# Two hybrid mixers: the second half's choice of keys cut in two round a recurrence step, later steps and splits in another order

## The chip, the cores and the metric

The kernel runs on one core of a Trainium2 chip. The core has five engines that run their own instruction streams and meet at semaphores: TensorE (PE, matmuls and transposes), VectorE (DVE), ScalarE (ACT), GpSimd (POOL) and SyncE (SP, which here only starts DMAs). The metric is the time of one execution in microseconds, lower is better; the figure compared is the median over runs.

## The reference

Two layers over 256 tokens of width 1024. Each layer has a mixer and a feed-forward part (dense SwiGLU in layer 0, top 2 of 8 experts in layer 1). The mixer projects the normed input, and feeds three branches whose outputs are gated and added:

```
proj = h @ w_in[layer]
a_u, a_b, a_c, s_u, q, k, v, qi, ki, wi, gates = split_columns(proj)
y_a = short_conv_mixer(a_u, a_b, a_c, conv_w[layer]) @ w_out_a[layer]
y_b = s5_mixer(s_u, ...) @ w_out_b[layer]              # diagonal complex recurrence, GELU, GLU
y_c = dsa_mixer(q, k, v, qi, ki, wi, ...) @ w_out_c[layer]
g = jax.nn.sigmoid(gates.reshape(Bsz, L, N_BRANCH, D_MODEL))
x = x + (g[:, :, 0] * y_a + g[:, :, 1] * y_b + g[:, :, 2] * y_c) @ w_o[layer]
```

In `dsa_mixer` a light indexer scores all keys for each query, the 64 best of the causal ones are chosen (`lax.top_k`), and attention with 8 heads runs over the chosen keys only. The kernel does this with a bias of -1e30 on keys that are not chosen.

## The kernel before

**Weights.** All weights pass as float32 chunks of 1 MB through three steps: SyncE loads a chunk into `raw` (6 buffers), ScalarE copies it to `w_hi` in TensorE's fp32r format (line 259, 3 buffers), and VectorE subtracts to get the rest `w_lo` (line 264). TensorE multiplies each chunk three times (hi by hi, lo by hi, hi by lo; lines 619 to 621, or 643 to 645 where channels stand on the partitions). A mixer has 35 chunks, numbered 0 to 34. Chunk n's matmuls wait for `lo_done` of n, ScalarE's copy waits for `used` of n - 3. "The split of chunk n" below is VectorE's instruction of line 264.

**Recurrence.** The S5 branch runs in 8 steps, q = 0 to 7. In each, TensorE makes the inputs (`bu`, lines 742 and 744; waits for `scanned` of step q - 1), VectorE rotates and scans them (`rotate_in`, called `turn_q`, lines 1634 to 1642; waits for the inputs, the step's table and the output of step q - 2), GpSimd rotates back (`rotate_out`, lines 2214 to 2217) and in mixer 0 then makes the table of step q + 2 (lines 2184 to 2190; in mixer 1 it loads it), and TensorE makes the outputs (`y_of`, lines 760 to 769; waits for `rotated`). `BU_AT` and `Y_AT` say behind which chunk TensorE places inputs and outputs of each step; at one chunk the output comes first. The last index in a list is step 7.

**Attention.** For each of two blocks of 128 queries VectorE searches the 64th best score in 8 rounds (`best`, lines 1707 and 1709), then marks the chosen keys and turns the marks into a bias in `keybias` (`choose`, lines 1717 to 1726, nine instructions). Four groups i = 0 to 3 (block i // 2, four heads each) go through `logits` (TensorE, line 810), `shift` (VectorE, lines 1740 to 1744; adds the bias), `softmax_exp` and `normalise` (ScalarE, lines 1248 and 1257, with VectorE's `invert_sums` between, line 1749), `turn_probs` (TensorE's transposes, line 822), `copy_pT` (ScalarE, line 1263), `values` (TensorE, line 833) and `copy_o` (ScalarE, line 1270).

**Gates.** `sigmoid_gate` (ScalarE, line 1241) puts a gate's half into `gate`, `merge_gate` (VectorE, line 1760) multiplies it with a branch's output. The tile `h_tok` holds the normed input, then the heads of q and k until they are turned (line 779), and from `merge_gate(layer, 0, ...)` on the merged output. For block 1, `best` and `choose` work in three rows of 256 columns: before, in the second half of `gate`.

**What sets the order.** Nothing but the code: each engine runs its instructions in the order in which the function of its block issues them. The functions `mixer` of TensorE, ScalarE and VectorE interleave chunk work with the steps above.

## Time and profile before

| | us |
|---|---|
| runs shown, median of 3 | 1796.02 (1794.18 to 1797.77) |
| profiled execution | 1792.95 |
| its span, first to last instruction | 1791.2 |
| TensorE busy | 1709.4 (95%) |
| VectorE busy | 1387.1 (77%) |
| ScalarE busy | 1069.8 (60%) |
| GpSimd busy | 394.3 (22%) |
| mean granted clock of TensorE | 0.979 of full speed |

Mixer 0 lies at about 0 to 287 us of the span, the dense part behind it, mixer 1 from about 490 to 740 us, and the experts from there to the end. Their second halves, from chunk 14 on, start at 129 and 617 us. The chain of work that ended last is 82% TensorE and 13% VectorE.

In a timeline row the columns are the start in us, the duration in us, engine, line, operation, tiles out and in, shapes and count; in brackets the engine's idle time before it and who ended it. VectorE's and TensorE's instructions overlap a little with the next, so the cost of a piece is taken from start to start.

### The profile page before, as it was taken

The numbers are of one execution on the slowest core, as the hardware profiler recorded it, in microseconds if no ns is written. First come the engines' busy times: TensorE is split into PE (matmuls) and PEld (weight loads), VectorE is DVE, ScalarE is ACT, GpSimd is POOL, SyncE is SP. The second block draws the span as 40 slices with busy tenths as digits, with TensorE's granted clock in tenths as the row PEclk, the third lists the DMA queues.
The fourth block names the chain that finished last, engine by engine and source line by source line (L and its number), as shares of the span: only waits on it lengthen the run. The fifth ranks groups of instructions, "written<-read, shape, count | busy, mean of one in ns | idle before, by whom it ended". The sixth has DMA issues, their size and how long they took to land.

```text
span 1791.2 us, 24481 instructions
## 1 busy us (share of the span) xinstructions
PE 1709.4 (95%) x9030; PEld 1446.3 (81%) x9030; DVE 1387.1 (77%) x1172; ACT 1069.8 (60%) x878; POOL 394.3 (22%) x492
## 2 busy tenths in 40 slices
PE   7898998999979989979999999999999999999998
PEld 5886887999868878767888888888888888888886
DVE  6987565455459875657888898898898988989987
ACT  5343454544343444446777777777777777777775
POOL 8978300899024332000000000000000000000000
PEclk9998999999989989979999999999999999999999
DMA  8432365556543434647999999999999999999995
GB/s 313 146 100 94 124 202 165 187 171 216 158 153 119 124 106 135 204 140 259 380 376 348 385 343 369 382 339 385 369 350 381 363 350 380 355 376 366 349 376 188
DMA packets 210840, 475.76 MB, mean 266 GB/s; under 512 B 7728, under 2 KB 32432, under 8 KB 210528
## 3 DMA queue, kind: packets, MB, share of 16 engines
q1 hardware_dynamic: 207456, 463.34, 73.1%
q0 software_dynamic: 2896, 11.01, 1.7%
q8 instruction: 36, 0.59, 0.1%
q10 hardware_dynamic: 432, 0.65, 0.1%
q14 instruction: 20, 0.16, 0.0%
HBM read 471.30 MB, written 3.67 MB: 265 GB/s over the span
## 4 chain that ended last, share of the span: by engine, by line
PE 82%; DVE 13%; issue 2%; ACT 2%; POOL 1%; DMA 0%; DVEq 0%; ACTq 0%; POOLq 0%
PE ps L619 24%; PE ps L621 23%; PE ps L620 23%; DVE w_lo L264 4%; PE ps L643 1%; PE ps L1073 1%; PE ps L644 1%; PE ps L645 1%; DVE x_tok L2077 1%; PE ps L742 1%; PE ps L744 1%; PE ps L767 1%; PE ps L685 1%; ACT w_hi L259 1%; PE ps L769 1%
## 5 line engine op out<-in xcount | busy, mean ns | idle before, releaser
L264 DVE TENSOR_TENSOR w_lo<-raw,w_hi 128x2048 fp32r<-128x2048 f32 (+1 forms) x439 | 1009.9, 2309 | 266.2 <-ACT w_hi L259 264.7
L259 ACT ACTIVATE w_hi<-raw 128x2048 fp32r<-128x2048 f32 (+1 forms) x439 | 839.5, 1915 | 377.6 <-PE ps L621 358.4
L619 PE MATMUL ps<-w_hi,xg_hi 128*128 128x512 f32 x896 | 358.2, 400 | 3.3 <-issue 1.4
L621 PE MATMUL ps<-w_hi,xg_lo 128*128 128x512 f32 x896 | 350.6, 391 | 0.0
L620 PE MATMUL ps<-w_lo,xg_hi 128*128 128x512 f32 x896 | 350.1, 391 | 0.0
L619 PE MATMUL ps<-w_hi,hT_hi 128*128 128x256 f32 (+2 forms) x672 | 228.1, 339 | 2.3 <-DVE hT_lo L1604 2.3
L620 PE MATMUL ps<-w_lo,hT_hi 128*128 128x256 f32 (+2 forms) x672 | 224.2, 334 | 0.0
L621 PE MATMUL ps<-w_hi,hT_lo 128*128 128x256 f32 (+2 forms) x672 | 224.1, 333 | 0.0
L619 PE MATMUL ps<-w_hi,hidT_hi 128*128 128x512 f32 x536 | 209.7, 391 | 2.8 <-DVE hidT_lo L1918 2.8
L621 PE MATMUL ps<-w_hi,hidT_lo 128*128 128x512 f32 x536 | 208.8, 390 | 0.0
L620 PE MATMUL ps<-w_lo,hidT_hi 128*128 128x512 f32 x536 | 208.7, 389 | 0.0
L619 PEld LDWEIGHTS ps<-w_hi,xg_hi 128*128 128x128 f32 x896 | 169.0, 189 | 43.4 <-DVE w_lo L264 8.6
L621 PEld LDWEIGHTS ps<-w_hi,xg_lo 128*128 128x128 f32 x896 | 168.7, 188 | 36.7
L620 PEld LDWEIGHTS ps<-w_lo,xg_hi 128*128 128x128 f32 x896 | 169.2, 189 | 32.9
L2316 POOL DMA_INDIRECT xg_tok<-table_store,token_of x7 | 18.8, 2679 | 783.2 <-DVE token_of L2041 783.2
L619 PEld LDWEIGHTS ps<-w_hi,hT_hi 128*128 128x128 f32 x672 | 128.1, 191 | 17.8 <-DVE hT_lo L1604 3.2
L621 PEld LDWEIGHTS ps<-w_hi,hT_lo 128*128 128x128 f32 x672 | 128.0, 191 | 12.3
L620 PEld LDWEIGHTS ps<-w_lo,hT_hi 128*128 128x128 f32 x672 | 128.3, 191 | 11.0
L619 PEld LDWEIGHTS ps<-w_hi,hidT_hi 128*128 128x128 f32 x536 | 100.7, 188 | 23.7 <-DVE hidT_lo L1918 3.3
L621 PEld LDWEIGHTS ps<-w_hi,hidT_lo 128*128 128x128 f32 x536 | 100.6, 188 | 21.1
L620 PEld LDWEIGHTS ps<-w_lo,hidT_hi 128*128 128x128 f32 x536 | 100.7, 188 | 20.3
L643 PE MATMUL ps<-hT_hi,w_hi 128*128 128x256 f32 x256 | 75.3, 294 | 6.3 <-DVE w_lo L264 6.3
(331 smaller groups left out, 2022.1 us busy)
## 6 DMA issues: line engine op xcount, KB each, us to landing
raw<-moe_w SPq DMA_DIRECT2D x336, 1024.0 KB, 7.2
raw<-w_in SPq DMA_DIRECT2D x44, 1024.0 KB, 5.4
raw<-ffn_w SPq DMA_DIRECT2D x33, 1024.0 KB, 5.3
raw<-w_o SPq DMA_DIRECT2D x8, 1024.0 KB, 5.0
raw<-w_out_a SPq DMA_DIRECT2D x4, 1024.0 KB, 5.0
raw<-w_out_c SPq DMA_DIRECT2D x4, 1024.0 KB, 5.0
raw<-w_out_b SPq DMA_DIRECT2D x4, 1024.0 KB, 5.0
raw<-w_in SPq DMA_DIRECT2D x4, 904.0 KB, 7.1
```

What stands on the lines that cost most here:

```text
L259: act.activation(w_hi[:, n % SPLIT, 0:width], raw[:, n % RAW, 0:width], ACT.Copy).then_inc(hi_done, 1)
L264: dve.tensor_tensor(w_lo[:, n % SPLIT, 0:width], raw[:, n % RAW, 0:width], w_hi[:, n % SPLIT, 0:width].bitcast(F32), ALU.subtract).then_in ...
L619: pe.matmul(dst, x_hi, hi, start=first, stop=False, skip_group_check=True)
L620: pe.matmul(dst, x_hi, lo, start=False, stop=False, skip_group_check=True)
L621: return pe.matmul(dst, x_lo, hi, start=False, stop=last, skip_group_check=True)
L643: pe.matmul(dst, wh, x_hi[:, k0 + k, :], start=start, stop=False, skip_group_check=True)
L644: pe.matmul(dst, wl, x_hi[:, k0 + k, :], start=False, stop=False, skip_group_check=True)
L645: mm = pe.matmul(dst, wh, x_lo[:, k0 + k, :], start=False, stop=last and k == 3, skip_group_check=True)
L685: tr = pe.transpose(ps[:, bank + k // 2, at:at + P], src[:, b, k * P:k * P + P], ident[:, :])
L742: pe.matmul(dst, ba[r:r + 32, c, part, :], u2[:, 0, :], start=part == 0 and jj == 0, stop=False, skip_group_check=True, tile_position=(r, 0))
L744: mm = pe.matmul(dst, b_rows[r:r + 32, c, part, :], u2[:, 1, :], start=False, stop=True, skip_group_check=True, tile_position=(r, 0))
L2316: pool.indirect_dma_start(xg_tok[:, :], None, h_rows, bass.IndirectOffsetOnAxis(token_of[:, 0:1], 0))\
```

## The change

The choice of block 1 is cut in two: `choose` keeps its first six instructions, and the last three move to a new function, `bias_of_choice`. Step 3 of the recurrence and the split of chunk 16 stand between them. Inputs and outputs of later steps go one or two chunks back on TensorE (tables `BU_AT`, `Y_AT`); the turned probabilities of groups 2 and 3 go behind another chunk or another step; ScalarE does two more splits and a gate ahead of softmax 2; the three choice rows of block 1 move from `gate` to `h_tok`, and with them the first search waits for `qkT_ps` (all heads turned) where it waited for `rope_done`. Both mixers run the same code.

```diff
-BU_AT = (10, 12, 13, 14, 15, 16, 17, 18)
-Y_AT = (13, 14, 15, 16, 17, 18, 19, 20)
+BU_AT = (10, 12, 13, 14, 16, 17, 19, 20)
+Y_AT = (13, 14, 15, 17, 19, 20, 21, 22)
...
 (TensorE, mixer)
                 rows(c0 + C_OA, 0, yac_hi, yac_lo, True, False, gates_read=6 * layer + 2)
-                turn_probs(layer, 2)
                 s5(C_OA)
                 rows(c0 + C_OA + 1, 2, yac_hi, yac_lo, False, True, block0=S["branch_block0"])
+                turn_probs(layer, 2)
+                s5(C_OA + 1)
                 values(layer, 2)
                 logits(layer, 3)
-                s5(C_OA + 1)
...
                 stripe(C_GC, 0, 1)
+                s5(C_GC + 1)
                 turn_probs(layer, 3)
-                s5(C_GC + 1)
...
 (ScalarE, mixer)
                 sp(16)
-                softmax_exp(layer, 2)
-                normalise(layer, 2)
                 sp(17)
                 sigmoid_gate(layer, C_GA + 2, 1, 1)
                 sp(18)
+                softmax_exp(layer, 2)
+                normalise(layer, 2)
+                sp(19)
                 copy_pT(layer, 2)
-                sp(19)
+                sp(20)
                 copy_o(layer, 2)
+                sp(21)
                 softmax_exp(layer, 3)
-                sp(20)
                 normalise(layer, 3)
-                sp(21)
+                sp(22)
                 copy_pT(layer, 3)
                 sigmoid_gate(layer, C_GC, 2, 0)
-                sp(22)
                 copy_o(layer, 3)
...
 (VectorE)
-                return (gate[:, r // 2, HALF + SEQ * (r % 2):HALF + SEQ * (r % 2 + 1)] for r in range(1, 4))
+                return (h_tok[:, 0, SEQ * r:SEQ * (r + 1)] for r in range(1, 4))
...
-                    dve.wait_ge(S["rope_done"], BLOCKS * (layer + 1))
+                    dve.wait_ge(S["qkT_ps"], 2 * (layer + 1))
...
                 own.then(dve.scalar_tensor_tensor(work, work, smalls[:, 1:2], eq, ALU.is_le, ALU.mult))
+
+            def bias_of_choice(b):
+
+                keys = (b + 1) * P
+                sc = keybias[:, b, 0:keys]
+                work, gt, _ = choice_rows(b)
                 own.then(dve.tensor_tensor(work, work, gt, ALU.add))
                 own.then(dve.tensor_scalar(sc, work, -NEG, NEG, ALU.mult, ALU.add))
...
                 choose(0)
+                bias_of_choice(0)
...
                 chunk(15)
-                choose(1)
-                chunk(16)
-                shift(layer, 2)
                 dve.wait_ge(S["ya_hi_done"], layer + 1)
                 sub_hi(flat(yac_lo[:, :, :]), flat(u_t[:, :, :]), flat(yac_hi[:, :, :]), S["ya_lo_done"])
+                choose(1)
+                turn_q(3)
+                chunk(16)
+                bias_of_choice(1)
+                shift(layer, 2)
+                chunk(17)
                 invert_sums(layer, 2)
-                turn_q(3)
-                chunk(17)
                 turn_q(4)
                 chunk(18)
                 add_skip(layer, 0)
                 add_skip(layer, 1)
+                merge_gate(layer, 0, C_OA)
                 turn_q(5)
-                merge_gate(layer, 0, C_OA)
+                chunk(19)
                 shift(layer, 3)
-                chunk(19)
+                chunk(20)
                 invert_sums(layer, 3)
+                chunk(21)
                 turn_q(6)
-                chunk(20)
+                chunk(22)
                 turn_q(7)
-                chunk(21)
-                chunk(22)
```

TensorE in mixer 0 behind the matmuls of chunk 15, before: the last output matmuls of step 2, then step 4's input matmuls (L742, L744), then chunk 16 (L619 on).

```order
L767 MATMUL ps<-state,ca 32x128
L769 MATMUL ps<-state,par_sb 32x128
L742 MATMUL ps<-su,ba 128x128 [waits scanned]
L744 MATMUL ps<-su,par_sb 128x128
L742 MATMUL ps<-su,ba 128x128
L744 MATMUL ps<-su,par_sb 128x128
L742 MATMUL ps<-su,ba 128x128
L744 MATMUL ps<-su,par_sb 128x128
L742 MATMUL ps<-su,ba 128x128
L744 MATMUL ps<-su,par_sb 128x128
L619 MATMUL ps<-w_hi,yac_hi 128x512 [waits lo_done,ya_lo_done,gate_done]
```

The same place of the changed kernel.

```order
L767 MATMUL ps<-state,ca 32x128
L769 MATMUL ps<-state,par_sb 32x128
L619 MATMUL ps<-w_hi,yac_hi 128x512 [waits lo_done,ya_lo_done,gate_done]
L620 MATMUL ps<-w_lo,yac_hi 128x512
L621 MATMUL ps<-w_hi,yac_lo 128x512
```

Step 4's input matmuls, which wait for step 3's scans, now stand behind the 24 matmuls of chunk 16.

VectorE in mixer 0 behind the split of chunk 15, before: the nine choice instructions, the split of chunk 16, then shift 2 (L1740 on).

```order
L264 TENSOR_TENSOR w_lo<-raw,w_hi 128x2048 [waits hi_done]
L1717 TENSOR_SCALAR gate<-keybias,top 128x256
L1718 TENSOR_SCALAR gate<-keybias,top 128x256
L1719 TENSOR_REDUCE row_sb<-gate 128x1 [waits dve_step]
L1720 SCALAR_TENSOR_TENSOR gate<-ones,gate 128x256
L1721 TENSOR_SCALAR row_sb<-row_sb 128x1 [waits dve_step]
L1722 SCALAR_TENSOR_TENSOR gate<-gate,row_sb 128x256 [waits dve_step]
L1723 TENSOR_TENSOR gate<-gate 128x256 [waits dve_step]
L1724 TENSOR_SCALAR keybias<-gate 128x256 [waits dve_step]
L1726 TENSOR_TENSOR keybias<-keybias,causal 128x128 [waits dve_step]
L264 TENSOR_TENSOR w_lo<-raw,w_hi 128x2048 [waits hi_done,dve_step]
L1740 SCALAR_TENSOR_TENSOR probs<-ps,keybias 128x512 [waits logit_ps]
```

VectorE in the changed kernel, from the sixth choice instruction on (L1722): step 3 (L1634 to L1642), the split of chunk 16, then the last three choice instructions (now L1729 to L1732).

```order
L1722 SCALAR_TENSOR_TENSOR h_tok<-h_tok,row_sb 128x256 [waits dve_step]
L1634 TENSOR_TENSOR qkT<-ps,table 128x4x128 [waits y_ps,bu_ps,table_done,dve_step]
L1635 TENSOR_TENSOR ps<-ps,table 128x512 [waits dve_step]
L1636 TENSOR_TENSOR ps<-qkT,ps 128x256 [waits dve_step]
L1637 TENSOR_TENSOR ps<-qkT,ps 128x256
L1642 SCALAR_TENSOR_TENSOR qkT<-trig,ps 128x128 [waits dve_step]
L1642 SCALAR_TENSOR_TENSOR qkT<-trig,ps 128x128 x3
L264 TENSOR_TENSOR w_lo<-raw,w_hi 128x2048 [waits hi_done]
L1729 TENSOR_TENSOR h_tok<-h_tok 128x256
L1730 TENSOR_SCALAR keybias<-h_tok 128x256 [waits dve_step]
L1732 TENSOR_TENSOR keybias<-keybias,causal 128x128 [waits dve_step]
```

Step 3 stood behind the choice, the split, shift 2, the split of y_a (`sub_hi`) and `invert_sums`; now only the split of y_a and six choice instructions stand between chunk 15's split and it.

ScalarE in mixer 0 behind the copy of chunk 16, before and then in the changed kernel.

```order
L259 ACTIVATE w_hi<-raw 128x2048 [waits used,raw_full4]
L1248 ACT_TABLE_LOAD
L1248 ACTIVATE probs,row_sb<-probs,row_sb 128x256 [waits shifted]
L1248 ACTIVATE probs,row_sb<-probs,row_sb 128x256 x3
L1257 ACTIVATE probs<-probs,row_sb 128x256 [waits row_inv_done]
L1257 ACTIVATE probs<-probs,row_sb 128x256 x3
L259 ACTIVATE w_hi<-raw 128x2048 [waits used,raw_full5]
```

```order
L259 ACTIVATE w_hi<-raw 128x2048 [waits used,raw_full4]
L259 ACTIVATE w_hi<-raw 128x2048 [waits used,raw_full5]
L1241 ACTIVATE gate<-ps 128x2x512 [waits used]
L259 ACTIVATE w_hi<-raw 128x2048 [waits used,raw_full0]
L1248 ACT_TABLE_LOAD
L1248 ACTIVATE probs,row_sb<-probs,row_sb 128x256 [waits shifted]
```

The copies of chunks 17 and 18 no longer stand behind softmax 2.

## Rows read from the trace of the kernel before

**Rows 1.** Timeline of TensorE, mixer 0, chunks 15 and 16.

```profile
136.65 0.49 PE L742 MATMUL ps<-su,ba 32*128 32x128 f32 x2
...
138.66 0.50 PE L619 MATMUL ps<-w_hi,hT_hi 128*128 128x512 f32 x1
...
144.34 0.41 PE L767 MATMUL ps<-state,ca 128*32 128x128 f32 x2
...
153.74 0.79 PE L742 MATMUL ps<-su,ba 32*128 32x128 f32 x2 [7.47 <-DVE qkT L1642]
...
165.30 1.03 PE L822 MATMUL ps<-ident,probs 128*128 128x128 f32 x8
```

**Rows 2.** Timeline of TensorE, mixer 1, chunk 16 and behind chunk 17.

```profile
639.34 0.79 PE L742 MATMUL ps<-su,ba 32*128 32x128 f32 x2 [5.19 <-DVE qkT L1642]
...
650.47 1.04 PE L822 MATMUL ps<-ident,probs 128*128 128x128 f32 x8
...
661.00 1.58 PE L833 MATMUL ps<-probs,v_sb 128*64 128x128 f32 x16
...
664.12 0.72 PE L760 MATMUL ps<-su,k 128*128 128x128 f32 x4
```

**Rows 3.** Stretches: length, busy us by engine, granted clock, DMA share, GB/s.

```profile
153.70:162.30 8.60, 8.56 (x27) 7.28 (x28) 6.84 (x10) 4.11 (x3) 8.16 (x7) 0.50 0.36 122
...
74.00:81.00 7.00, 4.99 (x25) 5.02 (x26) 6.76 (x14) 2.04 (x2) 6.84 (x9) 0.54 0.56 180
123.50:130.00 6.50, 6.50 (x48) 5.52 (x49) 4.93 (x8) 5.34 (x4) 4.18 (x2) 1.00 0.17 27
```

**Rows 4.** Timeline of VectorE, mixer 0, behind chunk 15, and the two skips.

```profile
135.16 0.81 DVE L1717 TENSOR_SCALAR gate<-keybias,top 128x256 f32<-128x256 f32 x1
...
138.83 1.29 DVE L1723 TENSOR_TENSOR gate<-gate 128x256 f32<-128x256 f32 x1
...
142.13 2.66 DVE L264 TENSOR_TENSOR w_lo<-raw,w_hi 128x2048 fp32r<-128x2048 f32 x1
144.72 1.27 DVE L1740 SCALAR_TENSOR_TENSOR probs<-ps,keybias 128x512 f32<-128x512 f32 x2
...
147.74 1.21 DVE L1782 TENSOR_TENSOR yac_lo<-u_t,yac_hi 128x1024 fp32r<-128x1024 f32 x1
...
150.08 0.69 DVE L1634 TENSOR_TENSOR qkT<-ps,table 128x512 f32<-128x512 f32 x1
...
153.72 2.29 DVE L264 TENSOR_TENSOR w_lo<-raw,w_hi 128x2048 fp32r<-128x2048 f32 x1
...
168.24 0.87 DVE L1649 SCALAR_TENSOR_TENSOR su<-su,par_sb,ps 128x256 f32<-128x256 f32 x2 [4.80 <-PE ps L769]
```

**Rows 5.** Timeline of VectorE, mixer 1, the choice of keys.

```profile
622.87 1.27 DVE L1717 TENSOR_SCALAR gate<-keybias,top 128x256 f32<-128x256 f32 x1
...
627.36 0.42 DVE L1723 TENSOR_TENSOR gate<-gate 128x256 f32<-128x256 f32 x1
...
628.47 2.29 DVE L264 TENSOR_TENSOR w_lo<-raw,w_hi 128x2048 fp32r<-128x2048 f32 x1
```

**Rows 6.** Timeline of TensorE, mixer 0, three earlier short waits.

```profile
72.11 1.06 PE L779 MATMUL ps<-ident,h_tok 128*128 128x128 f32 x8 [2.48 <-POOL h_tok L2234]
...
76.01 0.55 PE L643 MATMUL ps<-hT_hi,w_hi 128*128 128x256 f32 x1 [2.84 <-DVE w_lo L264]
...
123.49 1.14 PE L810 MATMUL ps<-qkT 64*128 64x256 f32 x8 [1.61 <-ACT qkT L1270]
```

**Rows 7.** Timeline of GpSimd, mixer 0, end of the table of step 3.

```profile
137.52 0.99 POOL L2190 TENSOR_TENSOR table<-pool_t 128x256 f32<-128x256 f32 x1
```

**Rows 8.** Timeline of ScalarE, mixer 0, the probabilities of group 2.

```profile
150.18 1.70 ACT L1257 ACTIVATE probs<-probs,row_sb 128x256 f32<-128x256 f32 x4 [0.24 <-DVE row_sb L1749]
```

**Rows 9.** Timelines of ScalarE and VectorE, mixer 0, the search of block 1.

```profile
84.19 0.38 ACT L1355 ACTIVATE qkT<-ps 128x256 f32<-128x256 f32 x1 [8.15 <-PE ps L779]
...
85.62 0.42 DVE L1707 MAX8 top<-keybias 128x8 f32<-128x256 f32 x1
```

## The prediction

> **What bounds the kernel now.** I read the list of who waited for whom first, then TensorE's own order of time in the second half of both mixers, then the stretches by clock, and last VectorE's order of time behind the two waits found. In the first view the one large wait of TensorE inside the mixers' second half is that of the input matmuls of a recurrence step (line 742) for VectorE's scans (line 1642). It comes once in each mixer, at the same place, before step 4's input matmuls: 7.47 us in mixer 0 [rows 1] and 5.19 us in mixer 1 [rows 2]. Elsewhere there TensorE goes from one piece to the next, so in this half each us of its idle time is a us of the span, and VectorE's load counts only where TensorE asks for something that isn't there.
>
> Each wait has a tail. In mixer 0 the matmuls from 153.7 to 162.3 run at a granted clock of 0.50, the lower of the two levels, 1.2 GHz; mixer 1 has the same tail, seen by its durations. The price by starts: step 4's input matmuls and chunk 16's 24 matmuls take 165.30 - 153.74 = 11.56 us. Step 3's input matmuls and chunk 15, the same work at 2.4 GHz, take 144.34 - 136.65 = 7.69 us [rows 1]. So the tail costs 3.87 us in mixer 0, and in mixer 1 (650.47 - 639.34) - 7.69 = 3.44 us [rows 2].
>
> **Why TensorE waits there.** It stands before step 4's input matmuls at 153.74 - 7.47 = 146.27, and in mixer 1 at 639.34 - 5.19 = 634.15. VectorE has much before step 3's scans are done. From the end of chunk 15's split at 135.16 it does the choice of keys (to 142.13: 3.67 us for the first six instructions, 3.30 for the last three), chunk 16's split (2.59), shift 2 (144.72 to 147.74: 3.02), the split of y_a (1.21), a wait for ScalarE's exponentials, and step 3 (150.08 to 153.72: 3.64) [rows 4].
>
> **The change part by part.** Times are those of the profiled execution.
>
> Step 4's input matmuls go behind chunk 16, and step 3 on VectorE comes right behind the first six choice instructions. Both old waits go: 7.47 + 5.19 = 12.66 us, and with them both tails, 3.87 + 3.44 = 7.31 us. Together 19.97 us. What is late next?
>
> Mixer 0, chunk 16. TensorE asks for its split at 146.27. VectorE: 135.16, + 1.21 for y_a, + 3.67 for six choice instructions = 140.04, + 3.64 for step 3 = 143.68, + 2.2 to 2.6 for the split = 145.9 to 146.3. The table that step 3 multiplies by ends at 137.52 + 0.99 = 138.51 [rows 7], 1.5 us before it is asked for. So chunk 16 waits 0 to 0.1 us, or 0.8 if the six choice instructions take the 4.49 us of mixer 1 [rows 5]; I take 0.2.
>
> Mixer 0, chunk 17. TensorE asks at 146.4 + 5.68 (24 matmuls, 138.66 to 144.34) + 2.01 (step 4's input matmuls) = 154.1. VectorE goes on from 146.1 with the last three choice instructions (3.30), shift 2 (3.02) and a split (2.2): 154.6. These three took 3.30 us in mixer 0 and 628.47 - 627.36 = 1.11 in mixer 1 [rows 4, 5]; with 1.11 the wait is gone. The most is 3.30 + 3.02 + 2.6 - 7.69 = 1.2, however late chunk 16 was, since TensorE starts it when VectorE has it. I take 0.7.
>
> Mixer 1. VectorE leaves chunk 15's split at 622.87 and needs 1.2 + 4.49 (622.87 to 627.36) + 3.64 + 2.2: 634.4, against 634.15. Wait 0.25. Chunk 17: TensorE asks at 634.4 + 7.69 = 642.1; VectorE has 634.4 + 1.11 + 3.02 + 2.2 = 640.7, or 643.3 with 3.30 for the three and 2.6 for the split. Wait 0 to 1.2; I take 0.15.
>
> New waits in all: 0.2 + 0.7 + 0.25 + 0.15 = 1.3 us, between 0 and 0.8 + 1.2 + 0.65 + 1.2 = 3.9 (the 0.65 is the 0.25 with a split of 2.6). None is near the waits after which the clock fell. Behind a wait of 1.61 us, at 123.49, the clock stays at 1.00, while from 74 to 81, round the second of two waits of 2.48 and 2.84 us, it is 0.54 [rows 3, 6]. So no tail is charged.
>
> Turned probabilities behind chunk 17, and ScalarE's softmax behind chunk 18's split. Before, group 2's probabilities are ready at 150.18 + 1.70 = 151.88 [rows 8] and turned at 165.30: 13.4 us of cover. Shift 2 ends about 4.7 us later than before (152.4 for 147.7), and TensorE comes to the turning about 5 us earlier (154.8 + 5.6 = 160.4). Cover left: 3.7 us, so no cost. ScalarE's two table loads fewer in each mixer lie in its idle time: nothing.
>
> Outputs of steps 3 to 7 and inputs of 5 to 7 move one or two chunks back. They are as many as before and at full clock cost the same. Values of one group and logits of the next, with the small wait between them, are 664.12 - 661.00 = 3.12 us [rows 2], and the wait in it stays. The gate merge ahead of step 5: after chunk 17 TensorE does the turning (0.9), output 3 (1.9), input 5 (2.0) and the 3.12 us, and asks for the merge at about 168.3. VectorE has output 3 at 163.2, two skips in 0.87 and half of the merge, as wide as the split of y_a, in 1.2 [rows 4]: 165.3, cover 3.0. Then merge, step 5 and chunk 19's split end by 172.5 to 172.9; TensorE, past chunk 18, asks at 174.0: cover 1.1 to 1.5. It is the thinnest one left. Later steps have more.
>
> Choice rows in h_tok: the search for the second block's keys now waits for all heads to be turned. ScalarE's copy behind the last turning starts at 84.19, and VectorE gets to the search at 85.62 [rows 9]: 1.4 us of cover, cost nothing. Queued behind that wait are shift 0, the convolution's input and chunk 11's split.
>
> **Sum.** -19.97 + 1.3 = -18.7 us. The profiled execution of 1792.95 us (span 1791.2) becomes 1774.3. Everything behind mixer 1 is moved as a block: TensorE's largest other waits are in the norms and come along. The median of the runs shown lies 3.07 us above the profiled execution, so I forecast 1796.0 - 18.7 = 1777.3 us.
>
> **A rule beside the rows.** The same three choice instructions cost 3.30 us beside GpSimd's table work and 1.11 without it [rows 4, 5], and GpSimd is busy in mixer 0 all through the stretch. The Trainium skill (SBUF — State Buffer, Who interferes with whom) says that a VectorE instruction with two SBUF inputs and a GpSimd instruction that reads SBUF hold one pair of ports in turn, the later one blocked till the first ends. By that rule mixer 1's three instructions, which now follow a split during which GpSimd's rotation stands ready, would be held too: with the 3.30 there the sum would be -18.7 + 1.05 = -17.6 us, 1778.4. No row of before has these instructions at that place, so the trace can't say whether they meet.
>
> **Rivals.**
>
> A. The slowing beside GpSimd comes at each new place, and the waits before chunks 16 and 17 reach their bounds. In mixer 0 that is 0.8 + 1.2 = 2.0 us in two waits one after the other, and such a pair may bring a tail of 3.9 back, as the clock fell behind the pair of 2.48 and 2.84 us. For it: the 1.11 against 3.30. Against it: every instruction would have to meet its worst case. Price in mixer 0: 2.0 - 0.9 + 3.9 = 5.0 us, 1782.3. In both mixers: 1.85 - 0.4 + 3.4 = 4.9 more, 1787.2.
>
> B. The wait only changes its place: step 3 is held by its table or by step 1's output, and TensorE stops as long before chunk 16 as it did before step 4. Then nothing is gained: about 1796. Against it is the table's end at 138.51.
>
> C. Slower: VectorE becomes the bound from chunk 16 to chunk 19. TensorE then meets a wait over 2 us at chunks 16 and 17 of both mixers, and each brings its own tail where before there was one in each mixer. Four times (2.5 + 3.9) = 25.6 us against 19.97 saved: 1801.7. It decides at 20 / 4 - 3.9 = 1.1 us a wait if each had a tail; but at 1.61 us none came, so it needs waits beyond that at all four places, while their bounds are 0.65 to 1.2.
>
> D. No new wait at all and a run at the lower edge of the spread: 1796.0 - 20 - 2 = 1774.
>
> **How the numbers follow.** Forecast, 1774 to 1781: 0.77. A: 0.17. B: 0.03. C: 0.03. D is the forecast's lower edge. The range is 1773 to 1786: it takes in the bounds of the new waits, the runs' spread of 1.8 us to either side, and A in one mixer. What a measurement can tell from no change is 0.2%, 3.6 us. Faster: 0.77 + 0.17 = 0.94; same: 0.03; slower: 0.03.
>
> **What would show it.** In the changed profile no wait before step 4's input matmuls in either mixer; clock 1.00 from chunk 15 to chunk 19; short waits, under 1 us, for VectorE's split of chunk 17 in mixer 0. The stretch from chunk 14 to chunk 23 is shorter by 10.4 us in mixer 0 and 8.2 in mixer 1. The forecast is wrong if a wait over 2 us with a clock of 0.5 stands before chunk 16 or 17, if the wait for the scans reappears at step 5 or 6, or if the dense or expert stage takes another time than before.

## The result and the profile after

| | before | after |
|---|---|---|
| median, us | 1796.25 (1794.18 to 1797.77) | 1777.36 (1776.43 to 1778.07) |
| profiled execution, us | 1792.95 | 1776.91 |
| its span, us | 1791.2 | 1775.2 |
| mean granted clock of TensorE | 0.979 | 0.983 |

The ratio is 0.9894, with a 95% interval of 0.9882 to 0.9905. The median before is here taken over four runs; the forecast started from the 1796.02 of the three shown. The medians differ by 18.9 us; the forecast was 18.7, a median of 1777.3.

The list of who waited for whom, TensorE in the changed kernel. Columns: us in total, times, longest.

```profile
PE ps L685 <- DVE h_tok L1591: 27.3, 4, 10.0
PE ps L643 <- DVE w_lo L264: 6.2, 3, 2.8
...
PE ps L619 <- DVE w_lo L264: 2.6, 5, 1.0
```

The two waits of the input matmuls for the scans (7.47 and 5.19 us, [rows 1, 2]) are gone from it. The last line was 0.5 us in 3 waits before: these are the new waits for VectorE's splits. The first line (the norms) is in both kernels.

TensorE's timeline in the changed kernel, chunk 16 to the turning of group 2's probabilities: mixer 0, then mixer 1.

```profile
147.16 0.47 PE L619 MATMUL ps<-w_hi,yac_hi 128*128 128x512 f32 x1 [1.03 <-DVE w_lo L264]
...
152.78 0.49 PE L742 MATMUL ps<-su,ba 32*128 32x128 f32 x2
...
154.95 0.50 PE L619 MATMUL ps<-w_hi,yac_hi 128*128 128x512 f32 x1
...
160.57 1.04 PE L822 MATMUL ps<-ident,probs 128*128 128x128 f32 x8
...
626.26 0.47 PE L619 MATMUL ps<-w_hi,yac_hi 128*128 128x512 f32 x1 [0.67 <-DVE w_lo L264]
...
631.89 0.49 PE L742 MATMUL ps<-su,ba 32*128 32x128 f32 x2
...
634.43 0.50 PE L619 MATMUL ps<-w_hi,yac_hi 128*128 128x512 f32 x1 [0.47 <-DVE w_lo L264]
```

Step 4's input matmuls (152.78, 631.89) start with no wait, where [rows 1, 2] have 7.47 and 5.19 us. Chunk 16 waits 1.03 and 0.67 us, chunk 17 0.47 us in mixer 1. In mixer 0 it waits about 0.15: from input matmuls to chunk it is 154.95 - 152.78 = 2.17, where 138.66 - 136.65 = 2.01 is the plain length [rows 1]. The new waits add up to 2.3 us.

TensorE's clock in the same stretch of mixer 0 (PEclk, the third number from the end), behind the turnings of the merged output in mixer 0's last part, and in the same stretch of mixer 1.

```profile
147.00:155.00 8.00, 7.75 (x41) 6.36 (x41) 7.83 (x10) 3.48 (x10) 7.61 (x7) 1.00 0.37 131
155.00:163.00 8.00, 8.00 (x46) 6.77 (x47) 5.69 (x10) 4.88 (x7) 7.65 (x8) 1.00 0.50 155
257.00:261.00 4.00, 3.12 (x14) 2.32 (x12) 3.81 (x7) 2.11 (x5) 1.02 (x2) 0.63 0.42 146
626.00:644.00 18.00, 17.28 (x98) 14.47 (x99) 14.99 (x22) 10.29 (x17) 10.01 (x9) 1.00 0.54 173
```

Where [rows 3] have 0.50, there is 1.00. The clock stays at 1.00 from chunk 14 to the GLU in both mixers: both tails are gone with the waits.

**Where the time went.** Starts of the same piece in the two timelines, us:

| piece on TensorE | before | after | earlier by |
|---|---|---|---|
| chunk 14, mixer 0 | 129.08 | 128.94 | 0.14 |
| GLU (first L643 with yb_hi), mixer 0 | 237.84 | 227.38 | 10.46 |
| first chunk of the dense part | 301.27 | 291.58 | 9.69 |
| first chunk of mixer 1 | 511.08 | 501.06 | 10.02 |
| chunk 14, mixer 1 | 616.96 | 608.40 | 8.56 |
| GLU, mixer 1 | 723.02 | 706.84 | 16.18 |
| turning in the last norm | 782.06 | 767.41 | 14.65 |
| end of the span | 1791.2 | 1775.2 | 16.0 |

From chunk 14 to the GLU both mixers now take the same 98.44 us. That is 10.32 us less in mixer 0 and 7.62 in mixer 1, 17.9 in all. The remaining 1.9 us of difference against the span's 16.0 is the net of what three places outside the changed stretches lose (3.8 us) and others give back (1.8, most of it in the routing and the experts). At the three places both kernels have the same waits, and the clock differs. One is the row from 257 to 261 above: clock 0.63 behind the same four waits of up to 0.67 us at which the run of before kept 1.00. The second lies in mixer 1's first half, where the gain falls from 10.02 to 8.56: behind the same wait of 2.78 us the clock is 0.70 over 10 us (551 to 561) where before it was 0.83 (561 to 571). The third is behind the turnings of the merged output in mixer 1, 0.83 over 10 us where before had 1.00. A second profile of the changed kernel (experiment 5) has 1.00, 0.83 and 0.83 at the three places, so such losses differ from run to run at least in part. The medians, which do not hang on one run, differ by 18.9: the profiled run of before lies 3.3 us under its median, that of after 0.5 under its own.

### The profile page after: what moved, and what is told of

It is laid out like the page before. It is cut to its first block, busy times and chain, and to the rows that moved or that the text cites. A ratio compares the mean times of both kernels' runs of the same rounds, so it can differ in the third digit from the quotient of the medians.

```text
span 1775.2 us, 24479 instructions
## 1 busy us (share of the span) xinstructions
PE 1705.0 (96%) x9030; PEld 1442.4 (81%) x9030; DVE 1390.7 (78%) x1172; ACT 1064.8 (60%) x874; POOL 404.7 (23%) x492
## 3 DMA queue, kind: packets, MB, share of 16 engines
HBM read 471.30 MB, written 3.67 MB: 268 GB/s over the span
## 4 chain that ended last, share of the span: by engine, by line
PE 81%; DVE 13%; issue 2%; ACT 1%; POOL 1%; DMA 0%; DVEq 0%; ACTq 0%; POOLq 0%
PE ps L619 24%; PE ps L621 23%; PE ps L620 23%; DVE w_lo L264 5%; PE ps L643 1%; PE ps L1073 1%; PE ps L644 1%; PE ps L645 1%; DVE x_tok L2085 1%; PE ps L742 1%; PE ps L685 1%; PE ps L767 1%; ACT w_hi L259 1%; PE ps L769 1%; POOL trig L294 1%
## 5 line engine op out<-in xcount | busy, mean ns | idle before, releaser
L619 PE MATMUL ps<-w_hi,xg_hi 128*128 128x512 f32 x896 | 357.7, 399 | 3.3 <-issue 1.4
L619 PE MATMUL ps<-w_hi,hT_hi 128*128 128x256 f32 (+2 forms) x672 | 228.9, 341 | 2.2 <-DVE hT_lo L1604 2.2
L619 PE MATMUL ps<-w_hi,hidT_hi 128*128 128x512 f32 x536 | 209.6, 391 | 2.8 <-DVE hidT_lo L1926 2.8
L619 PEld LDWEIGHTS ps<-w_hi,xg_hi 128*128 128x128 f32 x896 | 168.9, 188 | 43.3 <-DVE w_lo L264 8.5
L619 PEld LDWEIGHTS ps<-w_hi,hT_hi 128*128 128x128 f32 x672 | 128.6, 191 | 17.5 <-DVE hT_lo L1604 3.0
L619 PEld LDWEIGHTS ps<-w_hi,hidT_hi 128*128 128x128 f32 x536 | 100.6, 188 | 23.7 <-DVE hidT_lo L1926 3.3
L643 PE MATMUL ps<-hT_hi,w_hi 128*128 128x256 f32 x256 | 76.0, 297 | 6.2 <-DVE w_lo L264 6.2
```

Source lines behind the costliest of these rows:

```text
L619: pe.matmul(dst, x_hi, hi, start=first, stop=False, skip_group_check=True)
L643: pe.matmul(dst, wh, x_hi[:, k0 + k, :], start=start, stop=False, skip_group_check=True)
```

## The experiments

**1. The tables alone, and the rest alone.** To the kernel before, only TensorE's new tables:

```diff
-BU_AT = (10, 12, 13, 14, 15, 16, 17, 18)
-Y_AT = (13, 14, 15, 16, 17, 18, 19, 20)
+BU_AT = (10, 12, 13, 14, 16, 17, 19, 20)
+Y_AT = (13, 14, 15, 17, 19, 20, 21, 22)
```

> The kernel before with nothing changed but the two lists that say behind which chunk TensorE does each step's inputs and outputs; VectorE's and ScalarE's orders are those of before. Theory (lists and VectorE's order are one thing): the 7.47 and 5.19 us waits and their tails go, but step 5 still stands ahead of the gate merge and steps 6 and 7 ahead of the splits of chunks 20 and 21, so TensorE waits about 0.9 us before step 4's inputs, 4.8 at chunk 18, 4.9 at chunk 20 and 5.8 at chunk 21 of each mixer, three of them with a tail of 3.5: some 27 us in place of 11, slower than before by 10 to 30 us, about 1820 us. Rival (moving step 4's inputs alone brings the gain): about 1780 us.

Measured: 1838.26 us (1837.93 to 1839.18), ratio 1.0241 (1.0224 to 1.0258). TensorE's waits in mixer 0, but for one of 5.98 us before chunk 21:

```profile
149.04 0.47 PE L619 MATMUL ps<-w_hi,yac_hi 128*128 128x512 f32 x1 [2.79 <-issue]
156.07 0.65 PE L619 MATMUL ps<-w_hi,yac_hi 128*128 128x512 f32 x1 [2.46 <-ACT gate L1241]
...
181.15 0.80 PE L619 MATMUL ps<-w_hi,hT_hi 128*128 128x512 f32 x1 [4.91 <-DVE h_tok L1760]
...
206.35 0.77 PE L619 MATMUL ps<-w_hi,hT_hi 128*128 128x512 f32 x1 [6.07 <-DVE w_lo L264]
```

And the changed kernel with the old tables:

```diff
-BU_AT = (10, 12, 13, 14, 16, 17, 19, 20)
-Y_AT = (13, 14, 15, 17, 19, 20, 21, 22)
+BU_AT = (10, 12, 13, 14, 15, 16, 17, 18)
+Y_AT = (13, 14, 15, 16, 17, 18, 19, 20)
```

> The changed kernel with only the two lists of before. Theory: no wait before step 4's inputs (step 3's scans end 2 us before they are asked for), but the outputs of step 3 are asked for before GpSimd has rotated (1 to 1.8 us), inputs of 5, 6 and 7 wait 1.5, 2.7 and about 6 us for scans that now stand behind the gate merge and more splits, with one or two tails: 1795 to 1812 us, no gain. Rival (VectorE's new order alone brings the gain): about 1780 us.

Measured: 1819.02 us (1817.01 to 1820.08), ratio 1.0129 (1.0112 to 1.0146). Its largest wait in mixer 0:

```profile
193.89 0.79 PE L742 MATMUL ps<-su,ba 32*128 32x128 f32 x2 [8.06 <-DVE state L1642]
```

The tables alone cost 43 us and the rest alone 24 (against 1795.19 for before in this comparison), and together they gain 19. Both expectations were too small. The first named the late items at chunks 18, 20 and 21 rightly (4.8, 4.9 and 5.8 us expected, 4.91, 6.07 and 5.98 found), but it missed chunk 16. In mixer 0 the split of y_a, still behind shift 2 on VectorE, ends at 147.73 + 1.21 = 148.94, and chunk 16 starts at 149.04: this is the wait of 2.79 us for which the profile names nobody. The next row, 2.46 us, is the gate's second half, which ScalarE does behind softmax 2. The sum of that expectation was off too, since 27 us in place of 11 in each mixer is 32 us and not 10 to 30. In the second kernel the scans of step 7 came 8.06 us late, where 6 was expected, an output waited 2.04 us that was not on the list, and the other waits there, 0.56 to 2.33 us, were within about 1 us of their prices. So in the first kernel each part of the new TensorE order meets a VectorE or ScalarE item that is still at its old place: the split of y_a, the gate, the merge (L1760), splits of chunks. In the second the scans of later steps are late. The parts of this change have no prices of their own that could be added. The sum in the prediction worked because it followed the final order on all engines.

**2. Is the tail the price of TensorE's own idleness?** The kernel before, with filler matmuls ahead of step 4's input matmuls. They write where nothing is read and compute nothing that is used:

```diff
+                    if c == 15:
+                        pe.wait_ge(S["gate_done"], 6 * layer + 1)
+                        for _ in range((58, 40)[layer]):
+                            pe.matmul(ps[:, 0, 0:SEQ], hT_hi[:, 0, 0:P], hT_hi[:, 1, :], start=True, stop=True,
+                                      skip_group_check=True)
```

> The kernel before with TensorE given matmuls that nobody reads (58 in mixer 0, 40 in mixer 1, 256 columns each, about 0.12 us each) right before step 4's inputs, where it stood idle for 7.47 and 5.19 us. Theory (the tail is the price of the idle time): the waits for the scans stay in sum, the granted clock behind them is 1.00, and the time falls by the two tails, 7.3 us, to 1789 us. Rival (the tail belongs to that stretch, not to the idle time, so that taking the wait away would not have taken it): no change, 1796 us.

Measured: 1789.25 us (1786.76 to 1790.35), ratio 0.9967 (0.9955 to 0.998).

```profile
153.59 0.49 PE L742 MATMUL ps<-su,ba 32*128 32x128 f32 x2 [0.39 <-DVE qkT L1647]
```

```profile
145.00:153.70 8.70, 8.31 (x69) 7.90 (x68) 7.46 (x15) 5.73 (x14) 5.04 (x7) 1.00 0.40 121
153.70:162.30 8.60, 8.60 (x50) 7.29 (x51) 7.96 (x10) 4.03 (x4) 8.36 (x5) 1.00 0.36 124
...
640.00:650.00 10.00, 10.00 (x52) 8.22 (x52) 5.90 (x11) 3.80 (x3) 8.99 (x10) 0.84 0.77 237
```

In mixer 0 the scans come no sooner (step 4 at 153.59 instead of 153.74), but behind them the clock is 1.00 where [rows 3] have 0.50. Step 4's input matmuls and chunk 16 take 161.18 - 153.59 = 7.59 us there: the tail of 3.87 is gone whole. In mixer 1 they take 646.38 - 637.17 = 9.21 us, 1.5 more than the 7.69 at full clock. The clock fell to 0.50 in the middle of chunk 16 (0.50 from 641 to 643; the last row has 0.84 over 10 us), though TensorE had had no wait above 0.22 us since the fillers began. So the fillers took 3.97 + 1.92 = 5.9 us off the two pieces, and 5.9 us is what the medians show against the 1795.19 of before in the same comparison, where 7.3 was expected. TensorE's idle time is the main cause of the tails, but it is not the only thing that can bring the half clock; what brought it in mixer 1 is open. Of the 20 us removed by the change, 12.7 were waiting and 7.3 tail by the durations.

**3. Is the cut of the choice needed?** The changed kernel with the choice in one piece again:

```diff
                 choose(1)
+                bias_of_choice(1)
                 turn_q(3)
                 chunk(16)
-                bias_of_choice(1)
```

> The changed kernel with the last three choice instructions right behind the first six again, ahead of step 3 and chunk 16's split. Theory: chunk 16's split comes 2.6 us later in mixer 0 and 3.4 in mixer 1, the short waits there grow from 1.03 and 0.67 to about 3.6 and 4.0 us, the one before chunk 17 (0.47 in mixer 1) goes, and a tail of 3.5 to 3.9 comes back in each mixer: 1789 us; without tails 1783. Rival (the cut is worth nothing, since what it moves only changes its place): 1777 us.

Measured: 1778.98 us (1778.57 to 1783.94), ratio 0.9909 (0.9892 to 0.9925).

```profile
151.57 0.47 PE L619 MATMUL ps<-w_hi,yac_hi 128*128 128x512 f32 x1 [3.58 <-DVE w_lo L264]
...
634.39 0.47 PE L619 MATMUL ps<-w_hi,yac_hi 128*128 128x512 f32 x1 [1.78 <-DVE w_lo L264]
```

```profile
151.60:160.00 8.40, 8.40 (x34) 6.70 (x35) 5.20 (x6) 4.83 (x13) 8.01 (x8) 0.80 0.61 197
634.40:643.00 8.60, 8.60 (x44) 7.12 (x45) 5.95 (x8) 5.88 (x14) 6.11 (x5) 1.00 0.65 201
```

In mixer 0 the wait came as expected (3.58 for 3.6 us). In mixer 1 it is 1.78 us and not 4.0: at this place GpSimd stands still, and the last three choice instructions take 628.45 - 627.34 = 1.11 us instead of the 3.42 that I had added. The waits before chunk 16 are thus 5.36 us instead of 1.70, those before chunk 17 (0.62) are gone in exchange, and of the expected tails there is 0.80 behind 3.58 us and nothing behind 1.78. The medians are 1.6 us apart (2.7 by the ratios, since the two were run in different comparisons), and the intervals of the ratios overlap: the cut saves waiting by the rows, its price in time isn't shown. The title's main edit is at most a small part of the gain; the moves around it carry it. The profiled run of this kernel is its slowest, 5 us above its others; why the others are that much faster is not settled, since only this one has a trace.

**4. ScalarE's new order.** The changed kernel, softmax 2 at its old place on ScalarE:

```diff
 (ScalarE, mixer)
                 sp(16)
+                softmax_exp(layer, 2)
+                normalise(layer, 2)
                 sp(17)
                 sigmoid_gate(layer, C_GA + 2, 1, 1)
                 sp(18)
-                softmax_exp(layer, 2)
-                normalise(layer, 2)
 (VectorE)
-                chunk(17)
                 invert_sums(layer, 2)
+                chunk(17)
```

> The changed kernel, but ScalarE does softmax 2 where it did before the change, between the copies of chunks 16 and 17, and VectorE inverts the sums ahead of chunk 17's split. Everything on TensorE and step 3 on VectorE stay as changed. Theory: the new place of ScalarE's softmax is a needed part of the change, since shift 2 now ends about 5 us later. Exponentials to 154.8, normalising to 156.7, copy 17 to 158.6, its split to 160.8, against 154.8 where TensorE asks: a wait of 6.0 us before chunk 17 in mixer 0 and about 6.3 in mixer 1, and behind each a tail at half clock of 3.4 to 3.9 us. That is 19 us more than the changed kernel: about 1796, all of the gain given back. Rival: the order on ScalarE is indifferent, since ScalarE is idle 40% of the time: 1777.

Measured: 1801.99 us (1801.23 to 1804.69), ratio 1.0036 (1.0022 to 1.0051). TensorE and ScalarE in mixer 0:

```profile
160.26 0.80 PE L619 MATMUL ps<-w_hi,yac_hi 128*128 128x512 f32 x1 [10.79 <-ACT gate L1241]
```

```profile
154.37 1.71 ACT L1257 ACTIVATE probs<-probs,row_sb 128x256 f32<-128x256 f32 x4 [0.25 <-DVE row_sb L1755]
155.98 1.90 ACT L259 ACTIVATE w_hi<-raw 128x2048 fp32r<-128x2048 f32 x1
157.89 1.28 ACT L1241 ACT_TABLE_LOAD   x1
159.18 1.02 ACT L1241 ACTIVATE gate<-ps 128x1024 f32<-128x1024 f32 x1
```

The order on ScalarE is far from indifferent: 24.6 us more than the changed kernel, above the kernel before. The wait, though, is not where I expected it. It stands in the middle of chunk 16, not before chunk 17. The second block's half of chunk 16 goes into PSUM that still holds the gate's second half, and TensorE may not touch it until ScalarE has read it (the last row, with its table load ahead). That gate stood behind softmax 2, which waits for shift 2, which now ends later. The wait that I expected lies hidden in this one: chunk 17's copy stood in the same queue, and its split ends at 157.90 + 2.37 = 160.3, where TensorE would have asked at about 154.8. Moving the gate alone would therefore not have been enough by these rows; that was not run. Mixer 1 has the same wait, 11.21 us. From the end of the wait to the next input matmuls chunk 16's second half takes 165.13 - 160.26 = 4.87 us in mixer 0 and 4.30 in mixer 1, where half of 5.68 is 2.84: tails of 2.0 and 1.5. Sum: 10.79 + 11.21 + 2.0 + 1.5 - 0.6 (chunk 17's waits, gone) = 24.9, measured 24.6.

**5. The new waits and the shared ports.** The changed kernel's VectorE in mixer 1, and GpSimd's rotation of step 3 beside it:

```profile
626.02 1.41 DVE L1729 TENSOR_TENSOR h_tok<-h_tok 128x256 f32<-128x256 f32 x1
627.47 1.17 DVE L1730 TENSOR_SCALAR keybias<-h_tok 128x256 f32<-128x256 f32 x1
628.67 0.73 DVE L1732 TENSOR_TENSOR keybias<-keybias,causal 128x128 f32<-128x128 f32 x1
629.44 1.29 DVE L1746 SCALAR_TENSOR_TENSOR probs<-ps,keybias 128x512 f32<-128x512 f32 x2
```

```profile
624.02 3.13 POOL L2222 TENSOR_TENSOR pool_t<-qkT,table 128x512 f32<-128x512 f32 x1 [4.12 <-DVE qkT L1642]
627.23 1.25 POOL L2223 TENSOR_TENSOR qkT<-qkT,table 128x512 f32<-128x512 f32 x1
628.56 0.69 POOL L2224 TENSOR_TENSOR qkT<-qkT,pool_t 128x256 f32<-128x256 f32 x1
```

The last three choice instructions take 629.44 - 626.02 = 3.42 us here; before they took 1.11 [rows 5]. Each ends 0.15 to 0.3 us behind the GpSimd instruction beside it: 627.43 behind 627.15, 628.64 behind 628.48, 629.40 behind 629.25. To test it, GpSimd is held still in mixer 1 till shift 2 is done:

```diff
 (GpSimd, rotate_out)
                 pool.wait_ge(S["scanned"], 4 * (n + 1))
+                if layer == 1 and q == 3:
+                    pool.wait_ge(S["shifted"], 4 * layer + 3)
```

> The changed kernel, but in mixer 1 GpSimd starts its rotation of step 3 only when shift 2 is done, so GpSimd stands still while VectorE does the last three choice instructions. Theory (the two engines hold one another up): these three take 1.11 us, as they did before, and not the 3.42 us of the changed kernel, and TensorE's wait of 0.47 us before chunk 17 in mixer 1 goes. Output 3, which needs the rotation, still comes in time. Rival (their place behind a split or the row tile in h_tok makes them slow): they still take about 3.4 us. Time as the changed kernel or 0.5 us less.

```profile
624.74 0.42 DVE L1729 TENSOR_TENSOR h_tok<-h_tok 128x256 f32<-128x256 f32 x1
625.20 0.29 DVE L1730 TENSOR_SCALAR keybias<-h_tok 128x256 f32<-128x256 f32 x1
625.52 0.29 DVE L1732 TENSOR_TENSOR keybias<-keybias,causal 128x128 f32<-128x128 f32 x1
625.85 1.29 DVE L1746 SCALAR_TENSOR_TENSOR probs<-ps,keybias 128x512 f32<-128x512 f32 x2
...
628.50 2.28 DVE L264 TENSOR_TENSOR w_lo<-raw,w_hi 128x2048 fp32r<-128x2048 f32 x1
```

The three take 625.85 - 624.74 = 1.11 us again, though they stand at the changed place and work in h_tok. From the first of the three to the end of chunk 17's split it is 630.78 - 624.74 = 6.04 us, 2.3 less than in the changed kernel, and TensorE's wait before chunk 17 in mixer 1 is gone. Median 1776.16 us (1774.42 to 1777.75), ratio 0.9899 (0.9882 to 0.9916). The changed kernel, run once more on the same chip:

> The changed kernel once more, as the one that the next three are compared with on the same chip. Expected: 1777.4 us and a ratio of 0.989 to the kernel before. In its profile the waits for VectorE's splits before chunks 16 and 17 come to about 1.2 us in mixer 0 and 1.1 in mixer 1.

It came to 1777.13 us (1776.5 to 1777.73), ratio 0.9901 (0.9885 to 0.9918). Its waits at these places are 1.03, 0.67 and 0.46 us. So holding GpSimd brings 1.0 us by the medians, where 0 to 0.5 was expected, and the ranges overlap; the mechanism is shown by the rows, its price in time isn't.

The Trainium skill (SBUF — State Buffer, Who interferes with whom) says that a VectorE instruction with two SBUF inputs contends with a GpSimd instruction that reads SBUF, and that the one that is issued later is blocked for the other's whole length. This trace agrees for the two of the three that have two SBUF inputs: 1.41 and 0.73 us beside GpSimd, 0.42 and 0.29 without. The middle one has a single SBUF input, which that sentence of the Trainium skill doesn't cover, and it was slowed as well, 1.17 us for 0.29.

**6. Two small repairs.** The split of y_a has the same trouble: it takes 1.75 us in mixer 0 and 2.21 in mixer 1 where I took 1.21. In mixer 0 of the changed kernel, with the GpSimd instruction during which it starts:

```profile
135.03 1.75 DVE L1788 TENSOR_TENSOR yac_lo<-u_t,yac_hi 128x1024 fp32r<-128x1024 f32 x1
```

```profile
133.03 2.67 POOL L2194 TENSOR_TENSOR table<-pool_t 128x256 f32<-128x256 f32 x1
```

It needs nothing that is late, so it can stand ahead of step 2:

```diff
                 chunk(14)
+                dve.wait_ge(S["ya_hi_done"], layer + 1)
+                sub_hi(flat(yac_lo[:, :, :]), flat(u_t[:, :, :]), flat(yac_hi[:, :, :]), S["ya_lo_done"])
                 turn_q(2)
                 chunk(15)
-                dve.wait_ge(S["ya_hi_done"], layer + 1)
-                sub_hi(flat(yac_lo[:, :, :]), flat(u_t[:, :, :]), flat(yac_hi[:, :, :]), S["ya_lo_done"])
```

> The changed kernel with the split of y_a moved from behind chunk 15's split to ahead of step 2. Theory: in the changed kernel the split of y_a takes 1.75 and 2.21 us where it stands, and all of it lies on the way to chunk 16's split, for which TensorE waits 1.03 and 0.67 us. Ahead of step 2 it has cover, so both waits before chunk 16 go, and what stands before chunk 17 doesn't grow by as much: 1.7 us less than the changed kernel at least, about 2.2 at most. Rival: VectorE is short of time over the whole stretch, and the wait only moves to chunk 15 or 17: no change, within 0.3 us in the profile. Medians will hardly tell the two apart; the waits in the profile will.

Measured: 1775.5 us (1772.63 to 1776.9), ratio 0.9887 (0.9869 to 0.9906). That is 1.6 us under the changed kernel of the same comparison, about what was expected, but the ranges overlap. TensorE has no wait of 0.2 us or more left before chunks 16 and 17 in either mixer. VectorE in mixer 1:

```profile
615.49 1.28 DVE L1717 TENSOR_SCALAR h_tok<-keybias,top 128x256 f32<-128x256 f32 x1
...
619.41 0.54 DVE L1722 SCALAR_TENSOR_TENSOR h_tok<-h_tok,row_sb 128x256 f32<-128x256 f32 x1
619.99 0.69 DVE L1634 TENSOR_TENSOR qkT<-ps,table 128x512 f32<-128x512 f32 x1
```

From chunk 15's split to step 3 it is now 619.99 - 615.49 = 4.50 us instead of 6.00 (614.32 to 620.32 in the changed kernel); in mixer 0 3.70 instead of 5.82. The split itself takes 2.21 us at its new place too, but there nobody waits for it. With the second repair, in mixer 1 alone the choice in one piece:

```diff
                 choose(1)
+                if layer == 1:
+                    bias_of_choice(1)
                 turn_q(3)
                 chunk(16)
-                bias_of_choice(1)
+                if layer == 0:
+                    bias_of_choice(1)
```

> Both small repairs: the split of y_a ahead of step 2, and in mixer 1 alone the last three choice instructions right behind the first six, where GpSimd stands still and they take 1.1 us. Theory: the waits before chunks 16 and 17 fall from 2.3 us in all to under 0.5, so about 1.8 to 2.2 us less than the changed kernel. Rival: a wait over 1 us comes back in mixer 1, since three more instructions stand ahead of step 3 and chunk 16's split: same time as the changed kernel.

Measured: 1774.61 us (1773.4 to 1776.8), ratio 0.9892 (0.9874 to 0.9909), 2.5 us under the changed kernel of the same comparison; a wait of 0.28 us is left before chunk 16 in mixer 1. The same kernel in the next comparison:

> The kernel with both small repairs once more, as the one that the next is compared with on the same chip. Expected: 1774.6 us.

It came to 1774.85 us (1773.42 to 1776.22), ratio 0.9884 (0.9868 to 0.9901).

**7. The tails elsewhere.** To that kernel, fillers ahead of the waits in the norms and the routing:

```diff
+            def filler(count, bank):
+                for _ in range(count):
+                    pe.matmul(ps[:, bank, 0:SEQ], hT_hi[:, 0, 0:P], hT_hi[:, 1, :], start=True, stop=True,
+                              skip_group_check=True)
+
             def norm_turn(i):
+                if i:
+                    filler((0, 33, 68, 34)[i], (0, 7, 0, 7)[i])
...
             def route():
+                filler(18, 7)
                 pe.wait_ge(S["picked"], 1)
...
+                filler(10, 7)
                 pe.wait_ge(S["slots_done"], 1)
```

> Both small repairs, and filler matmuls (256 columns, results read by nobody) ahead of TensorE's waits in the two middle norms, the last norm and the routing: 33, 68, 34, 18 and 10 of them, at 0.12 us each a little less than the waits of 4.30, 8.58, 4.43, 2.51 and 1.55 us. Theory: the half clock behind a wait is the price of TensorE's own idle time, at these places as in the recurrence. In the changed kernel the granted clock is 0.50 from 287 to 292, from 492 to 500 and about 0.51 from 780 to 792 us. With the fillers these stretches run at 1.00, and the four stretches give back about 2 us each, less what the next wait (for the turned input's rest) takes back: 4 to 8 us, 1767 to 1771. Rival: behind the norms VectorE's split of the turned input is the limit, not TensorE's clock; then the clock rises and a wait of as many us appears behind it: 1774.

Measured: 1770.05 us (1767.38 to 1771.06), ratio 0.9862 (0.9846 to 0.9879). That is 4.8 us less than without the fillers, and the ranges are apart. The norm behind the dense part and the routing, by stretches, without and then with fillers:

```profile
492.00:500.00 8.00, 2.59 (x12) 2.35 (x13) 2.80 (x4) 2.54 (x5) 0.40 (x1) 0.50 0.32 125
...
780.00:792.00 12.00, 10.17 (x39) 9.38 (x40) 3.75 (x4) 1.02 (x1) 0.00 (x0) 0.50 0.23 87
```

```profile
488.00:500.00 12.00, 10.74 (x90) 10.30 (x89) 4.87 (x9) 6.58 (x10) 0.58 (x1) 1.00 0.53 190
...
771.00:782.00 11.00, 9.19 (x74) 8.66 (x74) 7.88 (x34) 3.32 (x4) 0.00 (x0) 1.00 0.08 13
```

The clock is 1.00 where it was 0.50. Part comes back as waits, as the rival said. The turning in the norm now waits for the second block too:

```profile
496.81 1.09 PE L685 MATMUL ps<-ident,h_tok 128*128 128x128 f32 x8 [0.54 <-DVE h_tok L1600]
498.62 1.09 PE L685 MATMUL ps<-ident,h_tok 128*128 128x128 f32 x8 [0.72 <-DVE h_tok L1600]
501.07 0.47 PE L619 MATMUL ps<-w_hi,hT_hi 128*128 128x452 f32 x1 [0.48 <-DVE hT_lo L1613]
```

Both theories hold in part, and the 4.8 us lie inside the 4 to 8 expected. At 1770 us this is the fastest kernel of the study.

## Why the prediction was right, point by point

- **Both waits and both tails go.** Right, in the waits list and the clock rows. The price of the tails (7.3 us) holds by the durations of both kernels; the fillers, which left 1.5 us of it standing in mixer 1, gave 5.9.
- **New waits.** The kind and places were right, the size was not: 2.3 us instead of 1.3. In mixer 0 chunk 16 waits 1.03 us, where I took 0.2 with a bound of 0.8. The mis-sized terms are the split of y_a at 1.21 us and the six choice instructions at 3.67. From 135.03 to 140.85, 5.82 us pass instead of 4.88. In mixer 1 two errors half cancel: the split of y_a costs 2.13 us from start to start instead of 1.2, the six choice instructions 3.87 instead of 4.49, and the wait is 0.67 instead of 0.25. The 1.21 was read where the split started just before a GpSimd instruction (147.74 against 147.76, and it was GpSimd's that took 1.82 us instead of about 0.8). At its new place it starts at 135.03, inside a GpSimd instruction that runs from 133.03 to 135.70, and takes 1.75. In these rows the one that starts first keeps its time and the other is held up, and the bound that I gave took no account of it for this split.
- **The last three choice instructions.** In mixer 1 I took 1.11 us and they took 3.42; in mixer 0 I took 3.30 and they took 2.57 (146.94 to 149.51). The two errors hit chunk 17 in opposite senses: 0.47 us instead of 0.15 in mixer 1, 0.15 instead of 0.7 in mixer 0. The rule that I set beside the rows gave the right answer for these three in mixer 1. Its total of -17.6 us is nearer to the 17.9 found inside the two stretches than my -18.7, but partly by luck: it put 1.05 us more on chunk 17 of mixer 1, where only 0.32 more came, since shift 2 took 2.65 us there and not 3.02, and the split 2.29 and not 2.6. The rest of the missing microsecond came at chunk 16.
- **By stretches.** Predicted 10.4 and 8.2 us, found 10.32 and 7.62. From the parts: 11.34 - 1.18 = 10.16 and 8.63 - 1.14 = 7.49, so nothing large is missing. Outside them the dense part took 0.3 us less than before and the experts 1.4 us less, against my sign that they take the same time; the clock at the experts' start came back sooner (0.57 over 10 us from 785.35 where before it was 0.50 from 800). The forecast moved all of this as a block, and only the sum of gains and losses makes that nearly right.
- **The total.** 18.9 us by the medians for 18.7 is in part luck. The stretches give 17.9, and the rest is within the spread of the runs.
- **ScalarE's order at no cost.** The number was right, the reason incomplete. I named the softmax's cover (3.7 us) and the table loads, but not the gate's second half, which moved ahead of softmax 2. In the changed kernel this gate ends at 144.30 + 1.02 = 145.3, and TensorE asks for it in the middle of chunk 16, at 147.16 + 2.84 = 150.0. With softmax 2 left ahead of the gate and of chunk 17's copy the whole gain is lost (experiment 4). The gate is the item that I should have named as covered, by 4.7 us. The softmax's own cover was right: 160.57 - 156.77 = 3.8 us for the 3.7 forecast.
- **The covers of the merge, of chunk 19's split and of the key search.** No wait appeared at any of them.
- **Rivals.** A's premise held (GpSimd slows VectorE at the new places), its tail didn't come: the two waits in mixer 0 are 1.03 and 0.15 us, and the clock stays at 1.00. B and C did not occur in the changed kernel. C's mechanism is what the tables alone show, with waits of 2.5 to 6.1 us for VectorE and ScalarE.

## What to carry to other kernels

Price a moved instruction not by its own duration at its old place, but by what runs beside it at the new one: for VectorE work on SBUF look at GpSimd's rows of the same moment. When a step is reordered on one engine, list for each thing that engine will now ask for sooner who makes it and what that maker has queued ahead; the reorderings on the other engines are often not side work but the condition. And where a long wait of TensorE can't be removed, harmless matmuls in it can give back the half-clock tail behind it: the whole 3.9 us in mixer 0, 1.9 of 3.4 in mixer 1.

## What the runs showed of the hardware

**The tail doesn't grow with the wait.** TensorE's waits and what followed:

| wait, us | where | behind it |
|---|---|---|
| 1.78 | choice whole, mixer 1 | clock 1.00 |
| 3.58 | choice whole, mixer 0 | clock 0.80 over 8.4 us, 1.6 us lost |
| 5.19 | before, mixer 1 | 3.4 us lost |
| 7.47 | before, mixer 0 | 3.9 us lost |
| 10.79 | softmax at its old place, mixer 0 | 2.0 us lost |
| 11.21 | the same, mixer 1 | 1.5 us lost |

Of the waits above 5 us the longest had the shortest tails. There more of the half-clock time passed while TensorE stood anyway: the clock was at 0.50 already from 156 to the wait's end at 160.3, and in mixer 1 from 646 to 653.1, before only from 150 to 153.7. What decides the length was not tested. Four waits of up to 0.67 us had 1.00 in one run and 0.63 over 4 us in another, at the same place of the program, and in the filled kernel the clock fell in mixer 1 with no wait above 0.22 us ahead of it. A forecast of one tail is therefore good to a few us only.

**The hold-up is mutual.** GpSimd's first rotation instruction takes 3.13 us when it starts during VectorE's split, and the second, of the same shape, 1.25 us. It isn't that the first is always slow: in the kernel before the one that starts at 166.50, while VectorE stands still, takes 1.18 us.
